# Tokens loaded before the first weights, head queries from split operands, and keys and probability transposes in other places

## The reference

```python
def mla_project(x, pos, w_in, q_norm, w_q_up, kv_norm, w_uk):
    z = x @ w_in                                   # 1024 -> 384 + 256 + 32
    cq = rms_norm(z[..., :Q_LORA], q_norm)
    ckv = rms_norm(z[..., Q_LORA:Q_LORA + KV_LORA], kv_norm)
    kr = rope(z[..., Q_LORA + KV_LORA:], pos)
    q = (cq @ w_q_up).reshape(B, L, N_HEADS, QK_NOPE + QK_ROPE)     # 16 heads, 64 + 32
    q_rope = rope(q[..., QK_NOPE:], pos)
    ...
```

## Time and profile before

| | us |
|---|---|
| median of 3 runs | 1406.89 |
| lowest and highest | 1406.12, 1407.55 |
| the profiled execution | 1406.64 |
| span in its profile | 1404.8 |
| start to the last product of the first weights | 34.8 |
| values and latent outputs, from 62.4 to the first head query product | 24.9 |
| one turn of the head loop (two heads) | 20.94 |

### The profile page before, as it was taken

How to read it: one execution, slowest core, us unless ns; L and a number is a source line. 1 busy time by engine, 2 the same in 40 slices (tenths; PEclk the granted TensorE clock), 3 DMA queues, 4 the chain that set the end, 5 groups by cost and what they waited for, 6 DMA issues and landing times.

```text
span 1404.8 us, 26582 instructions
## 1 busy us (share of the span) xinstructions
PE 1379.1 (98%) x10379; PEld 1283.5 (91%) x10379; DVE 639.1 (45%) x929; ACT 516.6 (37%) x832; POOL 232.3 (17%) x318
## 2 busy tenths in 40 slices
PE   9989999899999999999999999999999999999997
PEld 9847777557999999999999999999999999999996
DVE  3546666433572332223333678877522322333335
ACT  3236565423352221122221468854422211222234
POOL 0030010000551000000001525565600000000043
PEclk9999999999999999999999999999999999999999
DMA  8231110122233332232232222322333322322301
GB/s 220 65 91 28 24 28 19 60 87 94 61 90 91 90 105 90 60 90 80 75 119 76 68 68 69 92 78 74 95 90 101 103 81 60 89 77 85 123 1 64
DMA packets 180836, 111.14 MB, mean 79 GB/s; under 512 B 25896, under 2 KB 179069, under 8 KB 180768
## 3 DMA queue, kind: packets, MB, share of 16 engines
q1 hardware_dynamic: 180176, 109.41, 26.8%
q0 software_dynamic: 592, 0.79, 0.2%
HBM read 107.15 MB, written 3.02 MB: 78 GB/s over the span
## 4 chain that ended last, share of the span: by engine, by line
PE 91%; DVE 3%; ACT 2%; issue 1%; SPq 1%; POOL 0%; DMA 0%; DVEq 0%; ACTq 0%; POOLq 0%
PE ps L533 55%; PE ps L562 8%; PE ps L625 4%; PE ps L809 3%; PE ps L822 3%; PE ps L1165 2%; PE ps L845 1%; PE ps L1113 1%; PE ps L800 1%; PE ps L704 1%; PE ps L1000 1%; PE ps L955 1%; PE ps L1022 1%; PE ps L697 1%; PE ps L963 1%
## 5 line engine op out<-in xcount | busy, mean ns | idle before, releaser
L533 PE MATMUL ps<-xh,wl 128*128 128x280 f32 x1472 | 310.5, 292 | 0.0
L533 PE MATMUL ps<-xh,wh 128*128 128x280 f32 x1472 | 308.8, 291 | 0.7 <-ACT sg L1493 0.7
L533 PE MATMUL ps<-xl,wh 128*128 128x280 f32 x1472 | 307.9, 290 | 0.0
L1234 ACT ACTIVATE wh<-raw 128x2048 fp32r<-128x2048 f32 (+2 forms) x79 | 162.9, 2063 | 204.1 <-PE ps L533 179.3
L1583 DVE TENSOR_TENSOR wl<-raw,wh 128x2048 fp32r<-128x2048 f32 (+2 forms) x79 | 197.9, 2505 | 87.7 <-ACT wh L1234 87.6
L533 PEld LDWEIGHTS ps<-xh,wh 128*128 128x128 f32 x1472 | 233.9, 188 | 1.3 <-ACT sg L1493 1.1
L533 PEld LDWEIGHTS ps<-xh,wl 128*128 128x128 f32 x1472 | 234.6, 189 | 0.0
L533 PEld LDWEIGHTS ps<-xl,wh 128*128 128x128 f32 x1472 | 232.2, 188 | 0.0
L1920 DVE TENSOR_TENSOR ht<-sg,ps 128x560 f32<-128x560 f32 x44 | 32.5, 738 | 269.0 <-PE ps L533 264.8
L2111 POOL TENSOR_TENSOR acc<-xT 128x560 f32<-128x560 f32 x4 | 7.7, 1933 | 750.6 <-DVE xT L1806 648.5
L1495 ACT ACTIVATE hh<-ht 128x560 f32 (+1 forms) x44 | 29.6, 672 | 262.1 <-DVE ht L1920 262.1
(11 more groups left out here) (349 smaller groups left out, 2491.8 us busy)
## 6 DMA issues: line engine op xcount, KB each, us to landing
raw<-in_ffn_w_gu SPq DMA_DIRECT2D x176, 256.0 KB, 3.7
raw<-in_ffn_w_down SPq DMA_DIRECT2D x48, 384.0 KB, 4.3
raw<-in_lru_w_in SPq DMA_DIRECT2D x16, 512.0 KB, 4.5
Ctok<-in_cache_latent SPq DMA_DIRECT2D x48, 128.0 KB, 2.1
raw<-in_mla_w_o SPq DMA_DIRECT2D x16, 256.0 KB, 3.6
raw<-in_ffn_w_down SPq DMA_DIRECT2D x16, 256.0 KB, 5.0
raw<-in_lru_w_o SPq DMA_DIRECT2D x16, 256.0 KB, 3.3
wq<-in_mla_w_q_up SPq DMA_DIRECT2D x16, 144.0 KB, 2.4
```

The costliest lines, as they stand in the source:

```text
L533: mm = pe.matmul(ps[:, 1024 * jp + 512 * h:1024 * jp + 512 * h + TH], w[:, k, col:col + P], x[:, k, h * TH:(h + 1) * TH], start=(k == 0 an ...
L1234: act.activation(wh[u][:, 0:w], raw[u][:, 0:w], ACT.Copy).then_inc(hi_ok, 1)
```

## The change

Three parts, in one diff:

1. **Start.** Tokens are loaded first, the first weights behind them in pieces: rows k = 0, 1 (counted on `y_out`), k = 2, 3 (on `pg_in[5]`), k = 4 to 7 (on `raw_in[0]`). ACT and DVE split them piece by piece between and after the last token tiles. PE runs 14 products of ones in place of 51, transposes all 5 tiles, and does the first half of `first_part` in three stretches of k.
2. **Queries of the heads.** `z`'s query part is split once into `zqh` (ACT) and `zql` (DVE, in its place), and each head's `wq` into `wqh` and `wql` by POOL; `queries` does 9 fp32r products per half. The loop on POOL is written out, and four of the six pieces of latent output are issued behind the first two splits. `keys(0)` stands ahead of `queries(0)`.
3. **Inside the odd heads.** The transposes (0, 1), (0, 2), (1, 4), (0, 3) each stand one block earlier or later, and `keys(p + 1)` ahead of the last of them; ACT and DVE follow that order. The `V` stage uses the banks in another rotation.

Before, all six pieces of output went out ahead of the swaps; now two do, and the other four follow the split of the second head's weights. The diff, cut to its core:

```diff
@@ sync
-            load((KD, 256), lambda k0, k1: win[:, k0:k1, QL_R:QL_R + KV_R], 0, 0)
             sp.dma_start(ident[:], c_ident).then_inc(in_id, 16)
...
+            first = raw[0][:, 0:W_D].rearrange("p (k n) -> p k n", k=KD)
+            for k0, done in ((0, y_out), (2, pg_in[5])):
+                sp.dma_start(first[:, k0:k0 + 2, :], win[:, k0:k0 + 2, QL_R:QL_R + KV_R]).then_inc(done, 16)
+            for k in range(4, KD):
+                sp.dma_start(first[:, k, :], win[:, k, QL_R:QL_R + KV_R]).then_inc(raw_in[0], 16)
             load((KD, 256), lambda k0, k1: win[:, k0:k1, 0:256], 1, 1)
@@ tensor
             pe.wait_ge(s_ones, 4)
-            warm(38)
-            warm_wide(5, 512)
-            warm_wide(4, 280)
-            warm_wide(4, 256)
-
+            warm(14)
             pe.wait_ge(in_id, 16)
-            for t in range(4):
+            for t in range(5):
                 turn_x(t)
                 warm(4)
+            pe.wait_ge(s_xl0, 9)
+            for jp in range(2):
+                first_part(jp, 0, (0, 1))
+            pe.wait_ge(s_xl0, 12)
+            for jp in range(2):
+                first_part(jp, 0, (2, 3))
             pe.wait_ge(lo_ok, 1)
-            pe.wait_ge(s_xl0, 6)
-            first_part(0, 0, lambda k: turn_x(4) if k == 1 else None)
-            first_part(1, 0)
-            pe.wait_ge(s_xl0, 10)
+            for jp in range(2):
+                first_part(jp, 0, range(4, KD))
...
                 if n == 0:
-                    pe.wait_ge(wq_sw, h * 2 + 2)
+                    pe.wait_ge(wq_sw, h * 4 + 4)
                 for k in range(KQ):
-                    mm = pe.matmul(ps[:, 512 * n:512 * n + TH], wq[u][:, k, :], z[:, k, n * TH:(n + 1) * TH],
-                                   start=(k == 0), stop=(k == KQ - 1))
+                    for i, (w, x) in enumerate(((wqh, zqh[k][:]), (wqh, zql[:, k, :]), (wql, zqh[k][:]))):
+                        mm = pe.matmul(ps[:, 512 * n:512 * n + TH], w[u][:, k, :], x[:, n * TH:(n + 1) * TH],
+                                       start=(k == 0 and i == 0), stop=(k == KQ - 1 and i == 2))
...
                     scores(p, u, i)
-                    if u == 1:
-                        turn(p, *((0, 0), (0, 1), (0, 2), (1, 4), (0, 3))[n])
-                    elif not first:
+                    if i == 3 and u == 1 and not last:
+                        keys(p + 1)
+                    if i == 4:
+                        turn(p, 0, 0)
+                        turn(p, 0, 1)
+                    elif u == 1 and i > 0:
+                        turn(p, *((0, 2), (1, 4), (0, 3))[i - 1])
+                    elif u == 0 and not first:
                         turn(p - 1, 1, i)
...
+            pe.wait_ge(s_ve, 4)
+            pe.wait_ge(s_vd, 4)
+            keys(0)
             pe.wait_ge(s_lte, 6)
-            pe.wait_ge(s_z, KQ + KC)
+            pe.wait_ge(s_z, 2 * KQ + KC)
             for n in range(2):
                 queries(0, 0, n)
             pe.wait_ge(s_ve, 5)
             pe.wait_ge(s_vd, 5)
-            keys(0)
@@ scalar
+            def first_weights(piece):
+
+                act.wait_ge((y_out, pg_in[5], raw_in[0])[piece], (16, 16, 64)[piece])
+                at = slice(512 * piece, 512 * piece + 512 if piece < 2 else W_D)
+                act.activation(wh[0][:, at], raw[0][:, at], ACT.Copy).then_inc(s_xh0 if piece < 2 else hi_ok, 1)
...
+                if t >= 3:
+                    first_weights(t - 3)
+            first_weights(2)
...
+                if kt == 2:
+                    for k in range(KQ):
+                        act.wait_ge(s_z, KC + k + 1)
+                        act.activation(zqh[k][:], z[:, k, :], ACT.Copy).then_inc(s_zroot, 1)
@@ vector
+                if kt == 2:
+                    for k in range(KQ):
+                        dve.wait_ge(s_zroot, 3 + k)
+                        dve.tensor_tensor(zql[:, k, :], z[:, k, :], zqh[k][:].bitcast(F32), ALU.subtract).then_inc(s_z, 1)
...
+                if u == 1 and not last:
+                    read_k(p + 1)
                 normalise(p, u, 3)
                 if not last:
-                    if u == 1:
-                        read_k(p + 1)
                     read_q(h + 1, v)
@@ gpsimd
+            for t in range(2):
+                rows_out(t)
+
+            def swap(h, u):
 
                 pool.tensor_copy(wq[u][:, :, 96:112], wq[u][:, :, 80:96]).then_inc(wq_sw, 1)
                 pool.tensor_copy(wq[u][:, :, 112:128], wq[u][:, :, 64:80]).then_inc(wq_sw, 1)
+                pool.wait_ge(wq_sw, h * 4 + 2)
+                pool.tensor_copy(wqh[u][:], wq[u][:]).then_inc(wq_sw, 1)
+                pool.wait_ge(wq_sw, h * 4 + 3)
+                pool.tensor_tensor(wql[u][:], wq[u][:], wqh[u][:].bitcast(F32), ALU.subtract).then_inc(wq_sw, 1)
```

More of the change, by code:

```diff
@@ L188, in trunk @@
         rsum = put("rsum", [P, 6])
+        zql = place("zql", [P, KQ, T], F32R, reg)[0]
+        zqh = [place(f"zqh{k}", [P, T], F32R, at)[0] for k, at in enumerate((stat_at, ring_end - 3072, rt_at))]
+        wql = [place(f"wql{s}", [P, KQ, P], F32R, wq_at + 4 * KQ * P * s)[0] for s in range(2)]
+        wqh = [place(f"wqh{s}", [P, KQ, P], F32R, raw_at + 4 * (PAGES * KV_R + KQ * P * s))[0] for s in range(2)]
         Ctok = [put(f"Ctok{s}", [P, PAGES, KV_R]) for s in range(2)]
@@ L687, in turn_x, with first_part @@
                         mm.then_inc(s_xt, 1)
-            def first_part(jp, h, beside=None):
+            def first_part(jp, h, ks=range(KD)):
                 hi, lo = (w[0][:, 0:W_D].rearrange("p (k n) -> p k n", k=KD) for w in (wh, wl))
                 at = 1024 * jp + 512 * h
-                for k in range(KD):
-                    if beside is not None:
-                        beside(k)
+                for k in ks:
                     for n, (w, x) in enumerate(((hi, xh), (hi, xl), (lo, xh))):
@@ L770, in _ @@
                         pe.wait_ge(s_ve if g % 2 == 0 else s_vd, (g - 6) // 2 + 1)
-                    bank = 512 * (2 + (g + 2) % 6)
+                    if g == 2:
+                        pe.wait_ge(f1_ok, 3)
+                    bank = 512 * (2 + (g + 4) % 6)
                     for k in range(KC):
@@ L905, in head @@
                         queries(h + 1, v, 0)
-                    if i == 3 and u == 1 and not last:
-                        keys(p + 1)
                 if not last:
@@ L1341, in head @@
                     exp(p, u, i)
-                    if u == 1:
-                        read_pt(p, *((0, 0), (0, 1), (0, 2), (1, 4), (0, 3))[n])
-                    elif not first:
+                    if i == 3 and u == 1 and not last:
+                        read_k(p + 1)
+                    if i == 4:
+                        read_pt(p, 0, 0)
+                        read_pt(p, 0, 1)
+                    elif u == 1 and i > 0:
+                        read_pt(p, *((0, 2), (1, 4), (0, 3))[i - 1])
+                    elif u == 0 and not first:
                         read_pt(p - 1, 1, i)
@@ L2038, in _, with rows_out @@
                 pool.tensor_copy(K[s][64:P, :], krs[64:P, 0:NP]).then_inc(s_kp2, 1)
-            for t in range(6):
+            def rows_out(t):
                 pool.wait_ge(s_lte, t + 1)
@@ L2070, in _ @@
                 pool.wait_ge(wq_in[u], 16)
-                swap(u)
+                swap(u, u)
+            for t in range(2, 6):
+                rows_out(t)
             pool.wait_ge(s_ve, 5)
@@ L2077, in _ @@
             rotary(0, 0)
-            swap(0)
-            def head(h, u, more=True):
-                rotary(h, u)
-                if more:
-                    swap(u)
-                pool.wait_ge(o_sum, h * 2)
-                values(h + 1, 1 - u)
-            with pool.Fori(0, HEADS // 2 - 2) as i:
-                pool.wait_ge(wq_in[1], i * 16 + 32)
-                head(i * 2 + 1, 1)
-                pool.wait_ge(wq_in[0], i * 16 + 48)
-                head(i * 2 + 2, 0)
-            pool.wait_ge(wq_in[1], 16 * (HEADS // 2))
-            head(HEADS - 3, 1)
-            head(HEADS - 2, 0, False)
-            rotary(HEADS - 1, 1)
+            swap(2, 0)
+            for h in range(1, HEADS):
+                if h < HEADS - 2:
+                    pool.wait_ge(wq_in[h % 2], 16 * (h // 2 + 2))
+                rotary(h, h % 2)
+                if h < HEADS - 2:
+                    swap(h + 2, h % 2)
+                if h < HEADS - 1:
+                    pool.wait_ge(o_sum, h * 2)
+                    values(h + 1, 1 - h % 2)
             pool.wait_ge(q_sum, HEADS)
```

36 lines of the change are left out of this document (21 added, 15 removed).

## The result

The changed kernel takes **1398.47 us** in the median of 5 runs (1397.02 to 1401.11), where the kernel before takes 1406.12 (5 runs, 1405.65 to 1407.55). The ratio is 0.9947, interval 0.9934 to 0.9960: 0.5% faster. The prediction was 1393.5, from 1406.89 for the kernel before: 13.4 us less, and at least 8.4 by the upper end of its range, 1398.5. So the direction was right, but only 7.65 us came. The profiled execution took 1397.95 with a span of 1395.8, against 1406.64 and 1404.8 before: 9.0 us off the span, where 13.3 were forecast.

A forecast was written before the change was run, and what follows sets the result against it. PE, busy for 98% of the span, was taken to bound the kernel; start 5.5, values to heads 1.8 and loop 6.0 sum to 13.3 us off the 1404.8 span: 1391.5, so a time of 1393.5, range 1389 to 1398.5.

The forecast's parts named there:

- Part 1, the start: Kernel start: with tokens loaded first, the first-weight products end at 29.3 in place of 34.8, gaining 5.5 us.
- The second wait that was named: Start: PE was to wait twice, 0.4 to 0.9 us each, before the last product of the first weights.
- Part 2, values to heads: Between values and heads: POOL's splits just hidden by keys(0), the table load at 91.05 and not 92.84, gaining 1.8 us.
- Some 3.6 for issue, landing and two ACT copies: Values to heads: time added after POOL's two splits end at 84.2, giving 87.8, just hidden by keys(0).
- Part 3, even heads: Head loop, eight even heads: query products for both halves 0.52 us shorter per head, gaining 4.2 us.
- the products behind i = 4: Odd heads, first query half: PE has 1.62 us of work before the exponential's wait ends, as late as before: gain 0.
- Part 3, odd heads: Head loop, seven odd heads: only the second query half gains, 0.26 us each with keys earlier, 1.8 us in all.
- (a): Rival, loop gives little: DVE's normalisation and POOL's new operations hold each other up; 3 us less, 1396.5; chance 0.17.
- (b): Rival, start gives less: clock rises later or tokens land late; 3.8 in place of 5.5 us, 1395.2; chance 0.13.
- (c): Rival, loop gives all: both query halves count everywhere, 7.8 us, so 1391.7, or 1390 with a better start; chance 0.12.
- (d): Rival, slower: POOL's chain per head outgrows its 5 us cover, even heads wait 4 to 5 us, 1425; chance 0.03.
- (e): Rival, new query products not faster: at 0.158 us each and not 0.128, the 0.52 gain vanishes, 1400; chance 0.03.

The follow-up runs named there:

- e5: The changed kernel run once more, unchanged, for a second trace and more times: 1398.41 us, ratio 0.9943.
- e2: The changed kernel with the bank-7 half of keys first and the o_lo wait between the halves: 1394.35 us, ratio 0.9915.
- e8: e2 with the old fp32 query products, the amount of work on POOL and DVE kept: 1401.43 us, ratio 0.9954.
- e7: e2 with POOL casting each head's query weights three times in place of once: 1401.75 us, ratio 0.9955.
- e6: e2 with the second batch of cached pages issued inside the first two turns of the head loop, behind its weight loads: 1393.81 us, ratio 0.9909.
- e9: e6 plus 34 unread transposes where PE waits for ACT at the end of the head loop: 1392.88 us, ratio 0.9898.

## Why the prediction was wrong, point by point

- **Part 1, the start: right.** 5.62 came, with 5.5 forecast, through the steps as they were worked out: products of ones to 7.28 (7.4), first piece on ACT at 14.41 and on DVE to 15.75 (14.7 and 16.0), a wait of 0.54 ahead of the second piece (0.9), end at 29.20 (29.3). The second wait that was named is not in the timeline. Over eleven traces of kernels with this start the lead is 5.0 to 6.1, and two causes of the spread can be read from the chains of e5 (lead 6.1) and e2 (5.1):

```profile
1.45 5.36 PE ps L713 x28
```

```profile
4.84 10.07 DMA raw<-in_mla_w_in
```

  In e5 the products of ones are over at 6.81 in place of 7.28. In e2 the chain doesn't run through them: the first piece of the weights lands at 14.92, where some 13.7 was forecast, and ACT waits for it. So that the sum came out within 0.1 in the changed kernel's trace is in part luck.
- **Part 2, values to heads: mechanism right, one term too small.** "Some 3.6 for issue, landing and two ACT copies" counted some 2.2 us for the landing, as in the kernel before. It was 2.7 to 3.1, beside the page loads, both where PE waits for the buffers and at the last row (issued at 79.25, seen by ACT at 82.39). The cost of POOL's two operations was right (0.5 and 1.05 against 0.51 and 0.99), and with a landing of 2.0 so was the sum (1.86). Of the 1.8, 0.7 came, and 1.1 in e5.
- **Part 3, even heads: right.** 0.52 forecast, 0.60 measured, of which 0.51 are the products (8.49 in e8 against 7.98). That the products behind i = 4 give nothing in the odd heads was right too: from those scores to score 0 PE needs 2.81 both before (163.31 to 166.12) and in e2 (154.66 to 157.47).
- **Part 3, odd heads: this is the step that failed.** "`keys` come earlier, DVE reads them before its last normalisation, and the outputs find keys and probabilities there" looked at who waits for `keys`, and not at what `keys` itself waits for. Its second line is a wait for `o_lo`, and the transposes that were moved behind it had been its cover. Instead of 0.26 less, an odd head takes 0.19 more. A turn is 0.37 over the forecast, and the heads as a whole gave 4.0 us in place of 6.0. With the wait covered the turn would have been 19.99, 0.17 under the forecast: that is the part of the order in e8, which the prediction put at nothing.
- **Not foreseen at all**: 1.2 us of the profiled execution, by which of two engines gets through first at 932 us; and the falls of the clock, which put two of the five timed executions at 1400.7 and 1401.1; the median of the other three is 1397.95 and not 1398.47.
- **The rivals.** (a) is shown by e7 to be real; in the changed kernel it lengthens a normalisation by 0.2 to 0.4 us a turn and costs PE nothing that the trace shows. (b), in its full size of 1.7 us, was in none of the traces; in small it is the spread of the start, 0.5 us less in e2 by the late landing. (c), both halves everywhere, didn't happen. (d) is far: POOL's chain in e7 is 1.2 us longer and PE waits for no weights in the loop. (e) is out: 18 products take 2.50 with what follows, the six before took 2.93 (158.77 to 161.70).

On the span: 5.6 + 0.7 + 4.0 for the heads, less 1.2 in the recurrence, are 9.1, against 9.0 measured. Of the 4.3 that are missing from the forecast 13.3, 2.0 are the heads', 1.1 the stretch ahead of them and 1.2 the recurrence's. And 13.3, the forecast, is what e6 and e9 reach: their spans are 1391.6 and 1390.9 against the forecast 1391.5, with the two unforeseen costs of the new order taken away. That e6 comes so close is in part chance: each turn is 0.17 shorter than forecast, and the pages cost 0.8 in two of them. **e9 is the fastest of all**, with 1392.88 and a ratio of 0.9898; its distance from e6 and e2 is within the intervals.

## What to carry to other kernels

Before moving a block ahead of another, read the waits at its own head, and ask for each what ran beside it until now: the block that it is moved past may have been the cover. A buffer's second half that nobody waits for is a cheap place to put such a wait behind. And where an engine idles for a few microseconds between two full stretches, try filling it with work that nobody reads: here the clock fell behind such a stretch in some executions, at a cost of 2 to 5 us, and in none of the nine with fillers.

## What the runs showed of the hardware

- Two operations of DVE and POOL on SBUF that start together run one after the other: 2.29 and 1.39 alone, 2.29 and 3.55 or 3.53 and 1.39 together. They start within 0.04 us of each other in all thirteen traces; eleven have DVE first, two POOL, and the second outcome was worth 1.2 us at the end of the kernel. A normalisation beside POOL's subtraction is held for less: 0.66 in place of 0.49 where they overlap by 0.37 (e7).
- Behind the idle stretch at the end of the head loop (2.16 us of waiting in one piece, 1.15 and 0.80 beside it) PE's granted clock fell to 0.50 in five of eleven traces without fillers and stayed at 1.00 in the others, at a cost of 2 to 5 us; with 34 transposes into an unused bank nine of nine executions kept a mean of 0.998. Ahead of the loop, 2.51 us of waiting in one piece were followed by 0.58 (e7).
- Latent rows of 128 KB from POOL's queue land in 2.0 us (median) when SP has issued no pages near them. Beside the pages it is 2.0 to 2.2 in POOL's old order and 2.4 to 2.9 in the new one.
